# Quartered subtractions, a peeled last chunk, reordered routing and a token-major gather in a two-block MoE kernel

## What is computed

```python
# block 1
h = rms_norm(x, norm1_g) * (1 + sc1) + sh1
x = x + g1 * (mixed(h @ w_in) @ w_out)          # convolution and forgetting attention, gated
h2 = rms_norm(x, norm2_g) * (1 + sc2) + sh2
x = rms_norm(x + g2 * moe_ffn(h2), final_g)     # 32 experts, the best 4 for each token, 1024 -> 2048 -> 1024
# block 2
x = layer_norm_2(x, ln_emb_g, ln_emb_b)
for layer in range(2):
    mix = hybrid_mixer(x, w_in[layer], ...)     # windowed attention and two-way retention
    x = layer_norm_2(ALPHA * x + mix, ln1_g[layer], ln1_b[layer])
    if layer == 0: ffn = (silu(x @ w1) * (x @ w3)) @ w2     # 1024 -> 2816 -> 1024
    else:          ffn = moe_swiglu(x, ...)     # 8 experts, the best 2 for each token, 1024 -> 1408 -> 1024
    x = layer_norm_2(ALPHA * x + ffn, ln2_g[layer], ln2_b[layer])
```

## Time and profile before

| | |
|---|---|
| median of 3 executions | 2435.59 us (2433.46 to 2436.88) |
| profiled execution | 2436.44 us, span 2434.7 us |
| busy share of the span | PE 94%, DVE 31%, ACT 25%, POOL 14% |
| chain that ended last | PE 71%, DMA 11%, SP's queue 10%, DVE 4% |
| mean granted clock of PE | 0.966 |
| DMA | 688.61 MB, mean 283 GB/s |

### The profile page before, as it was taken

One profiled execution on the slowest core, in us unless ns is written; L12 is line 12 of the kernel. 1 busy time (PEld: TensorE's weight loads), 2 busy tenths in 40 slices (PEclk: granted clock), 3 DMA queues, 4 the chain that ended last, 5 costly groups with the idle time before them and its releaser, 6 DMA issues.

```text
span 2434.7 us, 35661 instructions
## 1 busy us (share of the span) xinstructions
PE 2299.7 (94%) x13682; PEld 1472.3 (60%) x13683; DVE 757.2 (31%) x1369; ACT 616.3 (25%) x889; POOL 350.0 (14%) x142
## 2 busy tenths in 40 slices
PE   5999899999999999999997999899899979999997
PEld 4887744444444444444446997899898865445444
DVE  6854332222222222222234344212324341111013
ACT  1143112111111111111124751433467011111111
POOL 1000000000000000000005632487475000000000
PEclk8999799999999999999997999899999979999999
DMA  9963389999999999989983433455363456899651
GB/s 371 369 220 106 87 337 418 418 417 418 418 418 418 418 418 418 418 339 418 418 322 117 141 87 121 156 191 174 104 191 105 171 191 260 352 407 397 266 237 65
DMA packets 226472, 688.61 MB, mean 283 GB/s; under 512 B 31386, under 2 KB 120418, under 8 KB 190562
## 3 DMA queue, kind: packets, MB, share of 16 engines
q1 hardware_dynamic: 221776, 685.82, 73.5%
q10 hardware_dynamic: 4626, 1.81, 0.3%
HBM read 686.53 MB, written 1.05 MB: 282 GB/s over the span
## 4 chain that ended last, share of the span: by engine, by line
PE 71%; DMA 11%; SPq 10%; DVE 4%; issue 2%; ACT 2%; ACTq 1%; POOL 0%; DVEq 0%; POOLq 0%
PE PS L982 16%; PE PS L645 12%; PE PS L656 11%; DMA RAW<-in_w_exp_in 9%; SPq L449 6%; PE PS L1078 6%; PE PS L946 4%; PE PS L1089 3%; PE PS L1268 3%; SPq L471 2%; PE PS L965 2%; DMA W<-in_moe_w 2%; PE PS L1042 2%; PE PS L700 1%; PE PS L742 1%
## 5 line engine op out<-in xcount | busy, mean ns | idle before, releaser
L982 PE MATMUL PS<-RAW,Z 128*64 128x512 f32 x3168 | 715.4, 598 | 24.6 <-DMA RAW<-in_w_exp_in 23.6
L397 POOL TENSOR_TENSOR WLO_D<-W,WHI_D 128x2048 fp32r<-128x2048 f32 x71 | 326.4, 4606 | 1240.0 <-ACT WHI_D L394 1240.0
L982 PEld LDWEIGHTS PS<-RAW,Z 128*64 128x64 f32 x3168 | 214.2, 137 | 457.0 <-issue 378.7
L1078 PE MATMUL PS<-W,Z 128*64 128x384 f32 (+1 forms) x1408 | 216.1, 464 | 9.0 <-DMA W<-in_moe_w 5.7
L1078 PEld LDWEIGHTS PS<-W,Z 128*64 128x64 f32 x1408 | 100.1, 138 | 126.4 <-issue 70.1
L656 PE MATMUL PS<-Z,W 128*128 128x256 f32 x768 | 174.1, 388 | 1.7 <-DVE Z L1867 1.5
L394 ACT ACTIVATE WHI_D<-W 128x2048 fp32r<-128x2048 f32 x71 | 135.3, 1907 | 120.2 <-DMA W<-in_ffn_w 48.5
L656 PEld LDWEIGHTS PS<-Z,W 128*128 128x128 f32 x768 | 149.1, 195 | 25.7 <-DVE Z L1867 1.9
L946 PE MATMUL PS<-Z 128*128 128x64 f32 x1088 | 128.6, 278 | 0.5 <-DVE Z L1972 0.5
L946 PEld LDWEIGHTS PS<-Z 128*128 128x128 f32 x1088 | 127.4, 196 | 0.9 <-issue 0.9
L1988 DVE TENSOR_TENSOR Z<-Z,PS 128x1024 f32<-128x1024 f32 x66 | 80.4, 1218 | 125.9 <-PE PS L965 125.9
(11 more groups left out here) (380 smaller groups left out, 2420.6 us busy)
## 6 DMA issues: line engine op xcount, KB each, us to landing
RAW<-in_w_exp_in SPq DMA_DIRECT2D x256, 1024.0 KB, 19.3
RAW<-in_w_exp_out SPq DMA_DIRECT2D x128, 1024.0 KB, 21.8
W<-in_moe_w SPq DMA_DIRECT2D x128, 704.0 KB, 15.2
W<-in_w_in SPq DMA_DIRECT2D x52, 1024.0 KB, 5.4
W<-in_moe_w SPq DMA_DIRECT2D x40, 1024.0 KB, 13.7
W<-in_ffn_w SPq DMA_DIRECT2D x33, 1024.0 KB, 5.2
W<-in_w_ada SPq DMA_DIRECT2D x24, 1024.0 KB, 13.4
W<-in_w_out SPq DMA_DIRECT2D x12, 1024.0 KB, 5.0
```

The lines of the kernel that those rows point to most:

```text
L397: eng.tensor_tensor(lo, raw, hi.bitcast(F32), ALU.subtract).then_inc(sem("dense_lo"), 1)
L982: mm = pe.matmul(ps(bank, 512, 64 * h, 64 * h + 64), x, w[:, c:c + 512], start=first, stop=final, skip_group_check=True)
L1078: mm = pe.matmul(ps(2 * i + b, n, 64 * h, 64 * h + 64), X1[:, s, :], first2(s)[:, c:c + n], start=(s == 0), stop=(s == 7), skip_group_chec ...
```

## The change

1. POOL's subtraction (L397) is made in four instructions of 128x512; the last one signals.
2. In the mixer of layer 0 POOL waits for `normed` 8 before its third subtraction.
3. `route`: all logits first; the transposes of the first 128 tokens stand behind them, those of the second behind the counts; the table's rows ahead of the gather instead of behind it. ACT loads the table of the exponential ahead, and takes the exponentials before both copies.
4. ACT's loop of the first expert stage runs to the last chunk but one; the last is written out and holds the first two splits.
5. Second expert stage: the gather makes XH2 token-major, four matmuls of 512 columns, PICK being the weights; ACT copies it, `turn_x` turns it by four transposes into bank 2, ACT copies X1. In the loop `turn_x` stands between the second products j = 3 and 4. The first products are 2 x 512, and 2 x 192 in one matmul of 384, instead of 2 x (384 + 320); the second products go to bank 3, the wait for `m2_ys_copied` stands ahead of the scatter. The hidden transposes are 4 and 1 instead of 3 and 2; silu and product are on 512 and 192 columns.

```diff
-                eng.tensor_tensor(lo, raw, hi.bitcast(F32), ALU.subtract).then_inc(sem("dense_lo"), 1)
+                for c in range(0, SLOT, 512):
+                    i = eng.tensor_tensor(lo[:, c:c + 512], raw[:, c:c + 512], hi[:, c:c + 512].bitcast(F32), ALU.subtract)
+                i.then_inc(sem("dense_lo"), 1)
...
                 for q in range(q0, q0 + 11):
+                    if q == 2:
+                        pool.wait_ge(sem("normed"), 8)
                     split_dense(pool, q)
...
-                    for k in range(KT):
+                    for h in range(2):
                         for a in range(2):
-                            mm = pe.matmul(ps(0, HALF, c0=k * HALF), HT[:, a, k * P:(k + 1) * P], PICK[:, a, 0:HALF],
-                                           start=(a == 0), stop=(a == 1))
+                            mm = pe.matmul(ps(0, 512, 64 * h, 64 * h + 64), PICK[:, a, 0:HALF], HT[:, a, 512 * h:512 * (h + 1)],
+                                           start=(a == 0), stop=(a == 1), skip_group_check=True)
                     mm.then_inc(sem("m2_gathered"), 1)
+
+                def turn_x(g1):
+
+                    pe.wait_ge(sem("m2_xh_copied"), g1)
+                    pe.nop(nofuse=True)
+                    for j in range(4):
+                        tr = pe.transpose(ps(2, P, c0=j * P), XH2[:, j * P:(j + 1) * P], IDENT[:, :])
+                    tr.then_inc(sem("m2_x_turned"), 1)
...
-                act.wait_ge(sem("route_x_turned"), m.nth)
-                tokens_first(0)
+                act.activation(SPARE[:, :], ONES[:, 0:1], ACT.Exp)
                 act.wait_ge(sem("route_top"), m.nth)
                 for a in range(2):
                     e = act.activation(GATE[:, a, 0:m.n], LOG[:, a, 0:m.n], ACT.Exp, bias=NTOP[:, a:a + 1])
                 e.then_inc(sem("route_gate_exp"), 1)
-                tokens_first(1)
+                for a in range(2):
+                    act.wait_ge(sem("route_x_turned"), 2 * m.nth - 1 + a)
+                    tokens_first(a)
...
+                last = act.value_load(TAB[0:1, LAST:LAST + 1], min_val=31, max_val=47)
+                with act.Fori(0, last) as g:
+                    chunk(g)
+                chunk(last, lambda: [split_dense(act, q) for q in range(2)])
                 turned(count)
```

More of the change, by code:

```diff
@@ L272, in build_two_blocks @@
         SIL2, HS2, HM2 = PART[:, 0:FH], HF[:, 0:FH], HF[:, FH:2 * FH]
+        XH2 = XG[:, 4:8, :].rearrange("p k c -> p (k c)")
+        X1H = X1.rearrange("p (h j) c -> p j h c", h=2)
         COUNT, LAST = 2 * P, 2 * P + 1
@@ L886, in route, with turn_tokens @@
                 ready, base = ("h_ready", 4) if m is m1 else ("stream_x", 12)
+                def turn_tokens(a):
+                    for k in range(KT):
+                        tr = pe.transpose(ps(4 + 2 * a + k // 4, P, c0=(k % 4) * P), x[:, k, a * P:(a + 1) * P], IDENT[:, :])
+                    tr.then_inc(sem("route_x_turned"), 1)
                 for k in range(KT):
@@ L891, in route @@
                         mm = pe.matmul(ps(a, E), x[:, k, a * P:(a + 1) * P], wr[:, k, :], start=(k == 0), stop=(k == KT - 1))
-                    for a in range(2):
-                        tr = pe.transpose(ps(4 + 2 * a + k // 4, P, c0=(k % 4) * P), x[:, k, a * P:(a + 1) * P], IDENT[:, :])
-                    if k == KT - 1:
-                        mm.then_inc(sem("route_logits"), 1)
-                tr.then_inc(sem("route_x_turned"), 1)
+                mm.then_inc(sem("route_logits"), 1)
+                turn_tokens(0)
                 pe.wait_ge(sem("route_mask"), m.nth)
@@ L904, in route @@
                     .then_inc(sem("route_counts"), 1)
+                turn_tokens(1)
                 if m is m1:
@@ L915, in route @@
                 mm.then_inc(sem("route_table_rows"), 1)
+                pe.wait_ge(sem("route_ht"), 2 * m.nth)
+                gather(1)
                 if m is m1:
@@ L1067, in first_product @@
                     pe.wait_ge(sem(f"raw{s}"), e * 32 + (raw1(s) + 32))
-                    for b, (c0, n) in enumerate(((0, 384), (384, 320))):
-                        for i in range(2):
-                            if s == 0:
-                                if i == 1 and b == 0:
-                                    pe.wait_ge(sem("m2_ys_copied"), g + 1)
-                                if i == 0:
-                                    pe.wait_ge(sem("m2_x_copied" if b == 0 else "m2_turned_copied"), g + 1)
-                            for h in range(2):
-                                c = 1408 * i + FH * h + c0
-                                mm = pe.matmul(ps(2 * i + b, n, 64 * h, 64 * h + 64), X1[:, s, :], first2(s)[:, c:c + n],
-                                               start=(s == 0), stop=(s == 7), skip_group_check=True)
+                    w = first2(s).rearrange("p (i n) -> p i n", i=2)
+                    for b in range(3):
+                        if s == 0 and b < 2:
+                            pe.wait_ge(sem("m2_turned_copied" if b else "m2_x_copied"), g + 1)
+                        for h in range(2):
+                            c = FH * h
+                            rhs = w[:, b, c:c + 512] if b < 2 else w[:, :, c + 512:c + FH]
+                            o = ps(b, 512 if b < 2 else 384, 64 * h, 64 * h + 64)
+                            mm = pe.matmul(o if b < 2 else o.rearrange("p (i n) -> p i n", i=2), X1[:, s, :], rhs,
+                                           start=(s == 0), stop=(s == 7), skip_group_check=True)
                     mm.then_inc(sem("m2_group_done"), 1)
@@ L1096, in turn_hidden @@
                     pe.nop(nofuse=True)
-                    for j in ((0, 1, 2), (3, 4))[part]:
+                    for j in ((0, 1, 2, 3), (4,))[part]:
                         tr = pe.transpose(ps(4 + j // 4, P, c0=(j % 4) * P), HS2[:, j * P:(j + 1) * P], IDENT[:, :])
@@ L1106, in experts2 @@
                 count = route(m2, X, WR2, gather)
+                turn_x(1)
                 with pe.Fori(0, count) as g:
@@ L1123, in experts2 @@
                             pe.wait_ge(sem("m2_hm_dve"), g + 1)
+                            turn_x(g + 2)
                         second_product(e, j)
@@ L1490, in experts1, with chunk @@
                 count = act.value_load(TAB[0:1, COUNT:COUNT + 1], min_val=32, max_val=48)
-                with act.Fori(0, count) as g:
+                def chunk(g, split=None):
                     turned(g)
@@ L1503, in experts2, with tokens_major @@
                 route(m2)
+                def tokens_major(g1):
+                    act.wait_ge(sem("m2_gathered"), g1)
+                    act.activation(XH2, ps(0), ACT.Copy).then_inc(sem("m2_xh_copied"), 1)
                 def tokens(g1):
-                    act.wait_ge(sem("m2_gathered"), g1)
-                    act.activation(X1, ps(0).rearrange("p (k c) -> p k c", k=KT), ACT.Copy).then_inc(sem("m2_x_copied"), 1)
+                    act.wait_ge(sem("m2_x_turned"), g1)
+                    act.activation(X1H, ps(2).rearrange("p (j h c) -> p j h c", j=4, h=2), ACT.Copy).then_inc(sem("m2_x_copied"), 1)
+                tokens_major(1)
                 tokens(1)
```

22 lines of the change are left out of this document (11 added, 11 removed).

## The result

The changed kernel takes 2405.09 us (median of 4, 2402.67 to 2406.26), beside 2435.85 us of the kernel before in the same comparison: 30.8 us less, a ratio of 0.9873 with a 95% interval of 0.9861 to 0.9885. The forecast was 2405.0 within 2393 to 2419.

A forecast was written before the change was run, and what follows sets the result against it. PE bounds the kernel: 71% of the chain of waits, busy 94% of the span. Terms 1.4 + 9 + 5.5 + 5.4 + 9.9 - 0.4 - 0.2 = 30.6 us off 2436.44 give 2405.8, median 2405.0, range 2393 to 2419.

The forecast's parts named there:

- POOL's quarters: POOL's 128x2048 subtraction in four pieces: 1.2 us each, 4.8 for four, at most 1.45 each; covered in the dense stages.
- T3: PE's only wait for a lo half from POOL, 1.0 us in all, was to grow by 0.2 to 0.4.
- C: Rival: POOL starts its next quarter before DVE gets in, so DVE still waits 4.9; 2411.5 us, chance 0.10.
- F: Rival, slower: in the dense stages a quarter costs over 1.44 us and POOL paces PE; 2446 us, chance 0.03.
- rival D: Gaps become so short that PE keeps full rate through T1, T2 and chunk 0; 2394 to 2399 us, chance 0.09.
- T2: Norm inside the first mixer of block 2 (1509 to 1530): shorter PE wait and less half rate, 5.5 us gained.
- T1: Handover from the first expert stage (1273 to 1317): splits moved ahead, DVE alternating with POOL's quarters; 9 us gained.
- Route 2: Second routing (1973 to 1999): gates 3.86 us sooner, shorter gather, first product at 1993.2 instead of 1998.63; 5.4 us gained.
- Route 1: First routing (282 to 309): same earlier gates, old gather stays, only the tail behind it shortens; 1.4 us gained.
- rival B: The gather's halves overlap only at the seam, losing 0.85 a chunk and 1.7 in route 2; 2411.6 us, chance 0.20.
- The second expert stage: Stage from 1999 to 2407: 1.7 us gained a chunk, swallowed by transfers in chunks 2 to 6; 9.9 us in all.
- signs of being wrong: L645 waiting for POOL often, the gather lasting over 2.5 us, or the squares still taking over 4.

## Why the prediction was right, and where it was not

**POOL's quarters, 1.2 us each: right in size.** 1.27 alone (5.06 for four), nearer the floor of 1.15 than the bound of 1.45, and covered in the dense stages. T3: PE's wait for POOL grew from 1.0 to 1.4, 0.4 as forecast. Rivals C and F fell: DVE does come in between quarters. Of rival D, T2 and chunk 0 of the second stage came true in the profile, T1 did not.

**T1, 9 forecast, 6.3 measured: the mechanism was right, its worth was not.** The forecast saw that POOL would meet the eight updates and hold five of them, and priced that at 4.6 for what follows; it was 3.9. It took PE's sums to be at full rate behind that (9.6, against 7.4 at half rate); they were not, behind a gap of 4.99 in PE which the text had not looked for. The other step that failed is the attribution: it took the moved splits and the quarters as one gain made by both, while T1 is 26.4 with quarters alone, 27.8 with the moved splits and no quarters, and 27.9 to 29.1 with both. That quarters alone gave the 9 is luck.

**T2, 5.5 forecast, 8.4 with the mixer around it: the terms were mis-sized.** 3.2 of 4.64 was to go and 4.25 did (0.39 is left). Of the half rate all went, not 2.3 of 2.8. That is 7.1, and record by record the two traces do draw apart by 7.1 from the start of the gap to the end of the half rate. The other 1.3 lies ahead of T2, where PE was at half rate for less time: 0.6 at the mixer's head, and 0.7 some 168 us into it, where the clock was at 0.5 for 6.8 us before and for 3.4 after.

**Route 2, 5.4 forecast, 6.8 measured.** The head gave its 3.9. The gather and what follows it were reckoned at half rate (3.4 and 1.0), and the clock rose meanwhile: 2.88 and 0.63. (The terms of the forecast add up to a first product at 1992.5; 0.7 of its 1993.2 has no term.) In the repeated profile of the changed kernel it didn't, and route 2 took 20.04, a gain of 5.5.

**Route 1, 1.4 forecast, 2.8 measured: mis-sized.** The forecast gave the tail behind the gather 1.4 and its start nothing. The gather starts 14.49 us after the first logit instead of 15.31, which is 0.8. From the end of the gather to the first product it takes 2.02 instead of 4.01, which is 2.0: the table's rows are made ahead of the gather, and the values are loaded beside it. PE at the end of route 1:

```profile
303.82 2.09 PE L932 MATMUL PS<-Z,W 32*128 32x256 f32 x16
305.84 4.09 PE L992 MATMUL PS<-RAW,Z 128*64 128x512 f32 x16
```

The first product stands right behind the last row of the bias, where 3.07 us lay between their starts before (305.80 and 308.87).

**The gather: right.** It runs in 1.88, so the halves overlap fully, and rival B fell. Eight records of 512 columns in 1.94 against 3.79 for 32 of 64. The forecast's 1.75 was an estimate, 4 x 0.43 for the case that the second half's matmuls overtake the first's; by its estimate for (B), with an overlap at the seam alone, the gather would take 2.6. What it read for this can be seen record by record in the trace of before. The second products of 512 columns on 64 columns' width start in pairs, 0.007 apart, from 2328.85 a pair every 0.43, so that both halves run at once; full-width records of 256 columns start one by one, every 0.216. The sixteen records on four row tiles start in fours within 0.02, at 305.80, 306.39, 306.82 and 307.24 (at half rate, granted clock 0.5): the first records of all four tiles run at once, ahead of every second one.

**The second expert stage, 9.9 forecast, 7.5 measured.** A chunk gained 1.1 instead of 1.7. The turn costs 0.74, not 0.5: four transposes take 0.59, and the rest, 0.15, goes to the second products around them. The gather gave 1.74, not 1.95: it took 1.88 and not 1.75, and the old one took 3.62 to its successor, where the prediction had read 3.72. The hidden transposes returned 0.06, not 0.22. Chunk 0 gave 2.8, of which 1.7 is the clock's. That the gain of chunks 2 to 6 would be swallowed was right, though it shows as a longer chunk 6 and not in each of them. Of chunk 7 the forecast kept most (0.8 of 1.7), and it gave 0.1.

**What the sum owes to chance.** Of the 2.1 us in the first expert stage 1.7 lie in its chunk 0, which took 16.8 us to its gather instead of 18.5, and 18.0 in the repeated profile of the changed kernel; chunk 0 of the second stage took 35.25, and 38.08 in the repetition, as before. Such differences between executions of one program are PE's rate, not the edit: the granted clock rose to 1.0 at 306.8 in the one and at 312.5 in the other, and in the second stage at 1969.0 and 1981.6. The median mixes such executions. It met the forecast within 0.1 us, and that is luck: of the seven stretches six were off by 1.4 to 2.9 us, in both directions.

**The signs.** Some did not come as written: a quarter takes 1.27 (1.15 to 1.25), the wait of 4.64 became 0.39 (1.5), the first product of the second stage comes 26.5 us earlier (21), a chunk takes 35.20 (34.6), the gather 1.88 (1.75). The wait of 7.90 came down to 1.97, as written, but the one of 2.04 ahead of it grew to 4.99. None of the signs of being wrong appeared.

## What to carry to other kernels

Where a VectorE instruction with two SBUF inputs waits for a GpSimd one (4.94 instead of 0.69 us here, behind subtractions of 4.6), cut GpSimd's instruction so short that the critical VectorE instructions wait for a piece of it (1.65 to 1.75 with quarters); but first ask whether it can be placed in VectorE's gap, which was worth 3 to 7 us more at T1 (22.34 and 23.03) than the cut alone (26.40), or than the cut with the splits moved (29.07). Moving work ahead to free one engine (ACT) moved its follower (POOL) onto another one's critical instructions (the eight updates took 8.41 instead of 3.26): follow each moved instruction to all that it releases. Two edits that aim at one wait do not add up; run each alone. Before a saving in a stage is added up, find the chunks that wait for transfers; here six chunks of eleven gained nothing in sum (224.89 against 225.14).
